# Triangular inverse per head in a 64x64 quarter of the TensorE array, with X and its transpose side by side

## What is computed

```python
def step(state, inp):
    rt, wt, kt, vt, kkt, at = inp
    sa = jnp.einsum("bhvk,bhk->bhv", state, -kkt)
    state = (state * wt[:, :, None, :] + sa[..., None] * (kkt * at)[:, :, None, :]
             + vt[..., None] * kt[:, :, None, :])
    return state, jnp.einsum("bhvk,bhk->bhv", state, rt)
```

## Time and profile before

| | us |
|---|---|
| median of 3 runs | 4256.69 |
| lowest, highest | 4254.74, 4256.97 |
| profiled execution | 4253.47 |
| its span | 4251.6 |

### The profile page before, as it was taken

How to read it: one execution, slowest core, us unless ns; L and a number is a source line. 1 busy time by engine, 2 the same in 40 slices (tenths; PEclk the granted TensorE clock), 3 DMA queues, 4 the chain that set the end, 5 groups by cost and what they waited for, 6 DMA issues and landing times.

```text
span 4251.6 us, 53880 instructions
## 1 busy us (share of the span) xinstructions
PE 3837.3 (90%) x21962; PEld 2283.9 (54%) x21962; DVE 1948.1 (46%) x4078; ACT 1429.4 (34%) x2596; POOL 139.9 (3%) x151
## 2 busy tenths in 40 slices
PE   2998899999899799999989879999999987999998
PEld 2554456556455356556546536556555644556554
DVE  7345554454245554454325464454442546454452
ACT  1333343343233233243224333343333333333242
POOL 0000000000000100000000010000000001000000
PEclk8998999999999899999999989999999998999999
DMA  7222110101212210110132120010012213010101
GB/s 308 60 88 63 32 32 26 31 31 41 84 47 91 65 37 26 32 31 22 42 98 61 60 81 26 27 33 25 31 56 74 61 60 86 27 31 26 32 31 40
DMA packets 269421, 229.01 MB, mean 54 GB/s; under 512 B 15548, under 2 KB 251256, under 8 KB 266104
## 3 DMA queue, kind: packets, MB, share of 16 engines
q1 hardware_dynamic: 266872, 217.18, 16.5%
q0 software_dynamic: 2304, 8.39, 0.5%
HBM read 208.76 MB, written 16.78 MB: 53 GB/s over the span
## 4 chain that ended last, share of the span: by engine, by line
PE 73%; DVE 15%; ACT 8%; issue 2%; DMA 1%; SPq 0%; DVEq 0%; ACTq 0%
PE bank L514 13%; PE bank L380 12%; PE bank L594 7%; PE bank L587 7%; PE bank L473 7%; PE bank L456 4%; PE bank L583 3%; PE bank L413 3%; PE bank L377 3%; DVE xm L1218 3%; PE bank L619 2%; PE bank L636 2%; PE bank L630 2%; PE bank L504 1%; DMA xm<-in_ada_w 1%
## 5 line engine op out<-in xcount | busy, mean ns | idle before, releaser
L514 PE MATMUL bank<-xm,wring 128*128 128x512 f32 x2048 | 1084.7, 631 | 68.8 <-ACT arena L876 35.4
L380 PE MATMUL bank<-arena,wring 128*128 128x512 f32 x1280 | 580.2, 593 | 14.0 <-ACT xm L722 10.2
L514 PEld LDWEIGHTS bank<-xm,wring 128*128 128x128 f32 x2048 | 336.0, 191 | 321.9 <-issue 174.8
L380 PEld LDWEIGHTS bank<-arena,wring 128*128 128x128 f32 x1280 | 230.8, 190 | 259.0 <-issue 254.4
L910 ACT COPY arena<-bank 128x512 f32<-128x512 f32 x320 | 187.5, 586 | 451.2 <-PE bank L583 451.2
L587 PE MATMUL bank<-arena 128*128 128x128 f32 x2560 | 338.1, 275 | 0.0
L594 PE MATMUL bank<-arena 128*128 128x128 f32 x2560 | 312.0, 275 | 0.0
L587 PEld LDWEIGHTS bank<-arena 128*128 128x128 f32 x2560 | 311.0, 192 | 0.0
L473 PE MATMUL bank<-wring,yT 128*128 128x512 f32 x608 | 277.6, 620 | 32.4 <-DVE yT L1251 22.3
L594 PEld LDWEIGHTS bank<-arena 128*128 128x128 f32 x2560 | 298.7, 192 | 0.0
L1326 DVE TENSOR_TENSOR arena<-bank,wmask 128x256 f32<-128x256 f32 x320 | 135.9, 425 | 302.4 <-PE bank L587 302.4
(11 more groups left out here) (256 smaller groups left out, 5026.1 us busy)
## 6 DMA issues: line engine op xcount, KB each, us to landing
wring<-in_rw_w_rkvz SPq DMA_DIRECT2D x128, 512.0 KB, 3.7
wring<-in_ev_w_in SPq DMA_DIRECT2D x96, 512.0 KB, 5.5
xm<-in_ada_w SPq DMA_DIRECT2D x16, 1536.0 KB, 12.3
wring<-in_ev_w_out SPq DMA_DIRECT2D x32, 512.0 KB, 8.0
wring<-in_rw_w_out SPq DMA_DIRECT2D x32, 512.0 KB, 3.5
xm<-in_x POOLq DMA_DIRECT2D x16, 512.0 KB, 5.7
arena<-in_x SPq DMA_DIRECT2D x16, 512.0 KB, 5.2
residual_scratch<-arena SPq DMA_DIRECT2D x4, 2048.0 KB, 7.5
```

The lines of the kernel that those rows point to most:

```text
L380: mm = pe.matmul(pj[:, :], w[:, k, :], hT[:, k, 1:1 + TB], start=(k == 0), stop=(k == KC - 1))
L514: mm = pe.matmul(pj[:, :], w[:, k, :], xmv[MIX_OF[i - 2]][:, k, :], start=(k == 0), stop=(k == KC - 1))
```

## The change

In place of block diagonal 128x128 matrices, each head's 64x64 matrix is used where it lies in r_Gs, on 64 partitions, and each matmul has 64 rows and 64 columns: one head works in one 64x64 quarter of the array and the other head in the opposite quarter. X and its transpose Y are kept side by side in r_XY; PE computes the updates of both, so that no transpose is needed after the first. Each level copies only one half of every block. DVE places the masked product into r_Q (a buffer a level, filled with identities once at setup) or into X with a predicated copy; ACT copies the updates of X and Y. GpSimd sets X to the identity before each unit. r_N, r_L, r_T, r_TT and the wmask table go. The last projection is no longer split around transposes and stands wholly before the inverse. In the chain, x is built on the opposite partitions, where Y is. New order on PE, one `rwkv_invert` per unit, with groups g of four chunks:

```diff
-                for h in range(2):
-                    rwkv_proj(b, pp, q, RN - KC + 6 + h, RN - KC + 7 + h)
-                    pe.wait_ge(S["r_n"], u * 2 + h + 1)
-                    for c in range(4):
-                        mm = pe.transpose(bank[h][:, c * P:(c + 1) * P], r_N[:, (4 * h + c) * P:(4 * h + c + 1) * P], ident[:, :])
...
-                for lv in range(5):
...
+                rwkv_proj(b, pp, q, RN - KC + 6, RN - KC + 8)
+                rwkv_invert(u)
+
+            def rwkv_invert(u):
+                def each(g):
+                    return [(c, h, half_of(1 - h), slice(c * 64, c * 64 + 64), (c - 4 * g) * 32)
+                            for c in range(4 * g, 4 * g + 4) for h in range(2)]
+                def product(g, m, rhs):
+                    for c, h, r, cc, at in each(g):
+                        n_c = r_Gs[r, gs_at(c, h):gs_at(c, h) + 64]
+                        mm = pe.matmul(packed(bank[g][r, at:at + 32], m), n_c, first(rhs[r, cc] if rhs is r_X else rhs[r, :], m),
+                                       start=True, stop=True)
+                    mm.then_inc(S["iq_ready"], 1)
+                for g in range(2):
+                    pe.wait_ge(S["sc_free"], u * 4 + 2 * g + 2)
+                    product(g, 1, ident64)
+                for g in range(2):
+                    pe.wait_ge(S["sc_free"], u * 4 + 4)
+                    pe.wait_ge(S["iq"], u * 12 + g + 1)
+                    product(g, 2, r_X)
+                    for c, h, r, cc, at in each(g):
+                        mm = pe.matmul(bank[2 + g][r, 2 * at:2 * at + 64], r_X[r, cc], ident64[r, :], start=True, stop=True)
+                    mm.then_inc(S["ixy_ready"], 1)
+                for lv in range(LV_INV):
+                    m = 2 << lv
+                    for g in range(2):
+                        pe.wait_ge(S["ixy"], u * 12 + 2 * lv + g + 1)
+                        if lv:
+                            product(g, m, r_X)
+                    for g in range(2):
+                        pe.wait_ge(S["iq"], u * 12 + 2 * lv + g + 3)
+                        if lv < LV_INV - 1:
+                            for c, h, r, cc, at in each(g):
+                                pe.matmul(packed(bank[2 + g][r, at:at + 32], m), r_Y[r, cc], first(r_Q[r, lv, cc], m), start=True, stop=True)
+                        for c, h, r, cc, at in each(g):
+                            mm = pe.matmul(packed(bank[2 + g][r, 128 + at:160 + at], m), r_Q[r, lv, cc], second(r_Y[r, cc], m),
+                                           start=True, stop=True)
+                        mm.then_inc(S["ixy_ready"], 1)
```

In the chain:

```diff
-                    pe.matmul(XB[r, 0:64], r_Gs[r, gs[h]:gs[h] + 64],
+                    pe.matmul(XB[half_of(1 - h), 0:64], r_Gs[r, gs[h]:gs[h] + 64],
...
-                    mm = pe.matmul(UZ[64 - 64 * h:128 - 64 * h, 0:64], r_T[r, c * P + 64 * h:c * P + 64 * h + 64], r_xs[r, :],
-                                   start=True, stop=True)
+                    s = half_of(1 - h)
+                    mm = pe.matmul(UZ[s, 0:64], r_Y[s, c * 64:c * 64 + 64], r_xs[s, :], start=True, stop=True)
```

On ACT, DVE and GpSimd, a unit's part of the inverse:

```diff
+                for g in range(2):
+                    act.wait_ge(S["ixy_ready"], u * 12 + g + 1)
+                    act.copy(r_Y[:, 256 * g:256 * g + 256], bank[2 + g][:, 0:256]).then_inc(S["ixy"], 1)
+                for lv in range(LV_INV):
...
+                        if lv < LV_INV - 1:
+                            act.copy(xy[:, :, 256 * g:256 * g + 256].rearrange("p z (a x m) -> p z a x m", x=2, m=m)[:, :, :, 0, :],
+                                     bank[2 + g][:, 0:256].rearrange("p (z a m) -> p z a m", z=2, m=m)).then_inc(S["ixy"], 1)
+                        else:
+                            act.copy(second(r_Y[:, 256 * g:256 * g + 256], m),
+                                     packed(bank[2 + g][:, 128:256], m)).then_inc(S["ixy"], 1)
```

```diff
+                def level(g, k, m, dst):
+
+                    V.wait_ge(S["iq_ready"], u * 12 + 2 * k + g + 1)
+                    V.copy_predicated(first(dst[:, 256 * g:256 * g + 256], m).rearrange("p (c a) m -> p c a m", c=4),
+                                      first(smask[:, k, :], m)[:, None].to_broadcast([P, 4, 32 // m, m]),
+                                      packed(bank[g][:, 0:128], m).rearrange("p (c a) m -> p c a m", c=4)).then_inc(S["iq"], 1)
+
+                V.wait_ge(S["x_set"], u + 1)
+                for k in range(LV_INV + 1):
+                    for g in range(2):
+                        level(g, k, 1 << k, r_Q[:, k - 1, :] if k else r_X)
```

```diff
+                for u in range(b * RP, (b + 1) * RP):
+                    gp.wait_ge(S["iq_ready"], u * 12)
+                    gp.tensor_copy(r_X.rearrange("p (c e) -> p c e", e=64), ident64[:, None, :].to_broadcast([P, NCH, 64]))\
+                        .then_inc(S["x_set"], 1)
```

More of the change, by code:

```diff
@@ L28 @@
 RN_CHAIN = 2 + 2 * KC + 2
+LV_INV = 5
+ARENA = 15136
 GROUPS = [(0, 1), (2,), (3,)]
@@ L126, in build @@
         gmask = sb("gmask", [P, 128])
-        wmask = sb("wmask", [P, 6, 128])
+        smask = sb("smask", [P, 6, 64], U8)
+        ident64 = sb("ident64", [P, 64])
+        r_Q = sb("r_Q", [P, LV_INV, NCH * 64])
         lmask = sb("lmask", [P, 8, 128], U8)
@@ L242, in gs_at, with first, second, packed @@
             return ((2 * (c // 4) + h) * 4 + c % 4) * P
-        def second_half(t, lv):
-            m = 2 << lv
-            return t.rearrange("p (c a x m) -> p c a x m", x=2, m=m, a=P // (2 * m))[:, :, :, 1, :]
+        def first(t, m):
+            return t.rearrange("p (a x m) -> p a x m", x=2, m=m)[:, :, 0, :]
+        def second(t, m):
+            return t.rearrange("p (a x m) -> p a x m", x=2, m=m)[:, :, 1, :]
+        def packed(t, m):
+            return t.rearrange("p (a m) -> p a m", m=m)
+        def half_of(h):
+            return slice(64 * h, 64 * h + 64)
         @block.sync
@@ L622, in rwkv_chunk @@
                 for h, r in heads:
-                    mm = pe.matmul(XB[r, 0:64], r_AR[r, a_c], Mcur[r, :], start=False, stop=True)
+                    mm = pe.matmul(XB[half_of(1 - h), 0:64], r_AR[r, a_c], Mcur[r, :], start=False, stop=True)
                 mm.then_inc(S["ch_x"], 1)
@@ L1011, in _ @@
                 own.wait()
+            own(V.tensor_tensor(ident64[:, :], m_t[:, 0:64], m_s[:, 0:64], ALU.is_equal))
+            own(V.tensor_tensor(i_x[:, 0:64], i_y[:, 0:64], i_s[:, 0:64], ALU.bitwise_xor))
+            own(V.tensor_tensor(m_le[:, 0:64], m_s[:, 0:64], m_t[:, 0:64], ALU.is_gt))
+            own.wait()
+            own(V.tensor_copy(m_x[:, 0:64], i_x[:, 0:64]))
+            own(V.tensor_copy(r_Q.rearrange("p l (c e) -> p (l c) e", e=64),
+                              ident64[:, None, :].to_broadcast([P, LV_INV * NCH, 64])))
+            own.wait()
+            step(V.tensor_tensor(m_x[:, 0:64], m_x[:, 0:64], m_le[:, 0:64], ALU.mult))
+            for j in range(LV_INV + 1):
+                step(V.tensor_scalar(m_ge[:, 0:64], m_x[:, 0:64], float(1 << j), None, ALU.is_ge))
+                step(V.scalar_tensor_tensor(out=smask[:, j, :], in0=m_x[:, 0:64], scalar=float(2 << j), in1=m_ge[:, 0:64],
+                                            op0=ALU.is_lt, op1=ALU.mult))
             own(V.tensor_scalar(i_r2, i_r, 63, None, ALU.bitwise_and))
```

88 lines of the change are left out of this document (17 added, 71 removed).

## The result

The changed kernel takes 4099.0 us (median of four runs, 4098.0 to 4104.3) against 4256.8 for the kernel before: ratio 0.963, 95% interval 0.962 to 0.964. That is 158 us less, where 252 were forecast; the time lies inside the range of 3930 to 4190. The profiled execution, the slowest of the four, took 4104.3 us with a span of 4102.5.

The account below looks back on a forecast made before the run. PE instructions, not hand-offs, were taken to bound the inverse: 15.4 us of instructions plus waits made 17.5 us, saving 7.85 us a unit, 251 us for 32. From 4253.5 us this gave 4002, as a median 4005; range 3930 to 4190.

Parts of the forecast that it names:

- the likeliest case: Whole kernel: cheaper inverse with the clock unchanged, 4005 us, by itself 3930 to 4060; chance 0.63.
- rival 1: Inverse on PE: a long stream issues more slowly than a burst, 0.041 us an instruction, 4160 us; chance 0.15.
- Spacing of the instructions: Inverse on PE: 512 small instructions at 0.030 us each, 15.4 us a unit.
- rival 2: Inverse on PE: two heads writing one bank do not overlap, 0.058 us an instruction, 4435 us; chance 0.07.
- Waits: Inverse hand-offs between PE, ACT and DVE left uncovered: 0.14 + 0.66 + 0.45 + 0.29 + 0.53 us a unit.
- Inverse: Stage from scores to chain: ends at 730.0 against 737.85, saving 7.85 us a unit, 251 us for 32.
- In the chain only output partitions change: nothing: Chain behind each inverse: moving output partitions changes no time; the chain should still take 30.9 us.
- Rival 3: Inverse and chain start: quarter-array work drops the clock to 1.2 GHz, 3 us a unit lost, 4360 us; chance 0.11.
- the sign of rival 3: RWKV layer: a granted clock under 1.00 in the timeline would show Rival 3.
- ACT's delayed Sigmoid: After ACT's last inverse copy: just fits, priced at nothing, up to 0.5 us a unit; blamed if chains grow a microsecond.
- GpSimd's reset: Reset of X once a unit: hidden, taken as zero, bound 0.8 us; blamed if chains grow a microsecond.
- Setup: Start of kernel: about 5 us of added work hidden under ada_w loads, taken as zero, at most 5 us once.

Follow-up runs that it names:

- wide: The changed kernel with every matmul of the inverse over all 64 data columns instead of 32, the rest going to unused bank columns; 3990.8 us, ratio 0.938.
- fill2: The changed kernel with the unit's last two projection matmuls moved from ahead of the inverse into its two uncovered waits; 4120.9 us, ratio 0.968.
- wide_early: As wide, but at level 0 the updates of group 0 wait only for their own group's transposes; 3976.2 us, ratio 0.934.
- wide_late_x: As wide_early, but GpSimd loads the next block's x only after the last product of the block's last inverse; 3969.0 us, ratio 0.932.

## Why the prediction was right in direction and too large in size

**Luck in the range.** The time is inside the stated range, but outside what the prediction gave the likeliest case by itself (3930 to 4060). The upper end of 4190 was there for rival 1, which did not happen; what filled that room is a cost that the sum did not have.

**Spacing of the instructions: right.** 0.030 us was taken; 0.029 was measured in the groups that no hand-off interrupts (the two heads' instructions start 0.007 us apart, a pair every 0.058). Rival 1 (0.041) and rival 2 (0.058) did not occur. The bank rule of the Trainium skill ("TensorEngine Tiling (Array Packing)", Gotcha 1) is contradicted by this trace: two heads on different row tiles write one bank and overlap through the whole inverse.

**Waits: half a microsecond too small, and hidden by the spacing.** The sum gave 17.5 us from the first product to the chain, and the timeline has 17.53 (699.66 to 717.19). That it is met so closely is luck: 512 instructions at 0.0292 are 14.9 us, not 15.4, and the time lost at hand-offs, counted as in the sum from the starts, is 2.6 us, not 2.07. It is 0.42 against 0.14 before the second product, 0.72 against 0.66 at level 0, 0.20 against 0.15 at each of levels 1 to 3, and nearly as forecast at the last level and the chain's start together (0.85 against 0.82). The idle times in brackets (0.23, 0.51, 0.37) are smaller, since they begin only when the last matmul has run out; the wait in the middle of the 32 products of a level has no bracket at all, but those take 1.13 us (708.49 to 709.62), not 0.93. The inverse started at 699.66, 1.91 us after the scores, as forecast.

The hand-off operations as measured, from the groups by line:

```profile
L1348 DVE COPY_PREDICATED r_Q<-smask,bank 128x128 f32<-128x128 uint8 x320 | 104.1, 325 | 387.4 <-PE bank L599 387.4
...
L935 ACT COPY arena<-bank 128x256 f32<-128x256 f32 x256 | 96.3, 376 | 288.2 <-PE bank L625 288.2
```

0.325 against the 0.35 taken, and 0.376 against 0.37.

**Inverse: 7.83 us saved in the unit shown, against 7.85.** Had nothing else happened, 32 units would give the 251 us of the sum.

**"In the chain only output partitions change: nothing": wrong.** The step was mis-sized at zero; it is 0.9 us a unit in our favour, 28 us. L619 and L626 stood in the rows with an even spacing of a pair of heads each, and I did not ask which quarters they share.

**The clock: this is the step that failed.** It stood among the rivals, as an alternative to the forecast with a chance of 0.11, not as a term of the sum. It took place together with the forecast: the inverse ran at full clock nearly everywhere, and the chain behind it paid. Rival 3 had the lower clock right and the place wrong. It put half of each inverse at 1.2 GHz (8.7 us of work) and 2.5 us into the chain; measured are 0.48 and 3.24 us. Its price of 11.2 us a unit was three times too large for that reason, which is why it forecast a slower kernel. Its reason, a quarter of the array per instruction, is not borne out as it stands: wide works on the same quarters and keeps the clock. The terms as they came out: 251 from the inverse, 28 from the chain, less 119 for the clock, less 3 for pauses, makes 157.

**A sign that pointed the wrong way.** The prediction named a granted clock under 1.00 in the RWKV stretch as the sign of rival 3, and it came (0.94). But it also said that a chain longer by a microsecond or more would mean ACT's delayed Sigmoid or GpSimd's reset. The chains are 2.3 us longer in the mean and neither is the cause: at full clock, with the Sigmoid and the reset in the same places, they take 30.75 us.

**Smaller points.** Setup: taken as hidden under the ada_w loads with at most 5 us; the first scores of the first block end 2.3 us later, and fill2, with the same setup, ends them 0.2 us earlier than the kernel before, so no price of setup is seen. GpSimd's reset takes 0.62 us and no DVE row beside it is longer. ACT's Sigmoid follows the last copy, as said (717.40 for the table load), and the chain of an undisturbed unit is not longer for it. The x load that slows PE in three inverses was not in the prediction at all; it cost 3 us.

## What to carry to other kernels

Packing small matmuls into quarters pays by the count of instructions times their spacing, and this spacing can be read from a burst of a few instructions; but ask what the clock does when a stage's instructions become light, and look for the price in the stage behind it. Where the spacing does not depend on the number of data columns, as with 32 and 64 here, more columns cost next to nothing (0.19 us a unit): here they brought another 108 us, on top of the 158 of the change. Count which quarters neighbouring matmuls share: exchanging two halves of an output was worth 28 us by itself.

## What the runs showed of the hardware that I had not expected

- The granted clock fell at the start of the chain, behind an inverse in which PE was busy 18.3 of 19.4 us, nearly all of it with 64x64 matmuls of 32 columns. The same instructions with 64 columns kept it at 1.00 in all 32 units.
- A 64x64 float32 matmul instruction costs 0.029 us in a stream whether it has 32 or 64 columns of data (two quarters in turn), and when all four quarters are in use twelve instructions go in 0.38 us.
- A projection matmul between groups of 64x64 matmuls costs 1.05 us to the next group instead of 0.86.
- A dense stream of small PE instructions pauses while a 2 MB load runs, for 0.43 to 2.02 us at a time in the changed kernel and 0.26 to 1.72 in wide, which the larger matmuls of before did not show: their last inverses are as long as the others (27.47 us). In wide_early and wide_late_x shorter pauses stand in other units too, without that load.
